# Folding the squares of five norms from four tiles to two on GpSimd, with half the ones-products, two k tiles later

## The chip, the cores and the metric

One core of one Trainium2 chip runs the program. The metric is the device time of one execution in microseconds (us), lower is better. Matrix products run on TensorE (PE in the rows), elementwise work on VectorE (DVE), ScalarE (ACT) and GpSimd (POOL), transfers are issued by SyncE (SP).

## The reference, cut to what matters

Six residual layers run over x of 256 tokens by 1024 features: conformer convolution, forgetting attention, short convolution, conformer convolution again, three attention branches with a gated mix, and a feed-forward layer. Each one norms x, computes, and adds to x:

```python
def rms_norm(x, g):
    xf = x.astype(jnp.float32)
    y = xf * lax.rsqrt(jnp.mean(xf * xf, axis=-1, keepdims=True) + NORM_EPS)
    return (y * g.astype(jnp.float32)).astype(x.dtype)
...
        if kind == 0:
            hn = rms_norm(x, a_norm[j])
            x = x + conformer_conv_mixer(hn, a_w_in[j], a_conv_w[j], a_conv_b[j],
                                         a_ln_g[j], a_ln_b[j], a_w_out[j])
```

What the change touches is `mean(xf * xf)`: a sum of squares over 1024 features for each of 256 tokens. There are six such norms. The first is computed apart; the other five stand at the borders between stages. They are numbered here by their phase: border 1 (into forgetting attention), 2 (into the short convolution), 3 (into the second conformer), 4 (into the three branches), 5 (into the feed-forward layer).

## The kernel before, in words

x is kept transposed in `xT` as eight tiles of 128 features by 256 tokens (k tiles 0 to 7), and worked on in four groups g of two tiles. Every product is made of three fp32r products: the weight is split into a high part `whi` and a low part `wlo`, x into `xh` and `xl`. The weights come in through a ring of three units. A unit is cut into halves; ScalarE makes a half's `whi` (L371), and either VectorE or GpSimd makes its `wlo` (L380). Which of the two it is stands in the half's record, by `cut` (a unit with `ALL` is VectorE's, otherwise the halves alternate). Each engine has its list of instructions in program order; what orders them against each other is semaphores.

At a border this happens. The last output unit's products (L884 to L886) end on TensorE. VectorE adds the result to x (L942) and then folds squares (`rms_fold`, L550: tiles 0 and 1 of `sqb` gather those of groups 0, 1 and 2). ScalarE squares each group (`rms_square`, L542) and makes `xh` of it (`raw_high`, L561); VectorE makes `xl` (`raw_low`, L566). TensorE meanwhile goes on with the next stage's first unit on the x that is not yet normed: `proj_raw` runs three products for each k tile (L752 to L754), after a wait for that tile's `xl`, in a first half (of eight k tiles) and a second one. The norm's factor is applied to the result later. In the middle of the first half stands `rms_pe`: the sum over partitions by fp32 products of a tile of ones with the squares (L720). Out of them ScalarE makes the root (`rms_act`, L697) and VectorE its reciprocal (`rms_dve`, L725), and with it `raw_scale` (L736) and `norm_dve_all` (L730).

Squares of four groups of two tiles are folded by VectorE into tiles 0 and 1; with tiles 6 and 7, the last group, that makes four tiles, and so four products:

```python
            for k in (0, 1, 6, 7):
                if k == 6:
                    pe.wait_ge(sq_done, 4 * ph + k // 2 + 1)
                mm = nc.tensor.matmul(rms_bank[ph][:, 0:S], ones, sqb[:, k, :], start=(k == 0), stop=(k == 7))
```

GpSimd's own list is short: the additions of eleven taps of each convolution (L1120, L1123), the gated product behind it (L1129), and `wlo` of the halves that are its own (`lo_pool_to`). `conf_pool` is its part of a conformer, and begins with `lo_pool_to(pool, last(n["vg"][0][1]))` (L1103), the low halves up to the conformer's first input unit.

Of the kernel before, what the change touches and what calls it, by code (L numbers as in the profile page):

```python
# [20 lines left out]
ALU = mybir.AluOpType  # L21
# [4 lines left out]
S = 256  # L26
TB = S // P
D = 1024
KD = D // P
# [74 lines left out]
def program(nc, t, out):  # L104
    ctx = ExitStack()
    with ctx:
        place = [(nc.sbuf_base + 31) // 32 * 32]

        def sb(name, cols, rows=P, dt=F32):

            at = place[0]
            place[0] += (4 * cols + 31) // 32 * 32
            return nc.alloc_sbuf_tensor_at(name, [rows, cols], dt, offset=at)
# [5 lines left out]
        def sem(name):  # L119
            return ctx.enter_context(nc.semaphore(name))  # L120
# [4 lines left out]
        ones = cst[:, C_ONE:C_ONE + P]  # L125
        blk64 = cst[:, C_B64:C_B64 + P]
        xT = sb("xT", KD * S)[:, :].rearrange("p (k t) -> p k t", t=S)
        sqb = sb("sqb", KD * S)[:, :].rearrange("p (k t) -> p k t", t=S)
# [112 lines left out]
        sq_done = sem("sq_done")  # L241
# [52 lines left out]
        halves = []  # L294
        splits = []
        n_hi = []
        first_half = []
# [19 lines left out]
        def hs(u):  # L317

            return range(first_half[u], first_half[u + 1] if u + 1 < len(first_half) else len(halves))

        def last(u):
            return hs(u)[-1]

        def is_split(h):
            return n_hi[h] > (n_hi[h - 1] if h else 0)
# [61 lines left out]
        def lo_pool_to(pool, h_last):  # L387
            lo_to(pool, nc.gpsimd, pool_at, False, lo_pool, h_last)
# [132 lines left out]
        def plan_ffn(ph):  # L521
            w = t["w_ffn_in_2"][0]
            n = {"ph": ph}
            n["gu"] = [(group((y_raw, 64 + i + 1)), unit_in(w, [(i * P, P), (FF + i * P, P)], ALL)) for i in range(KF)]
            n["out"] = plan_out_ffn(t["w_ffn_out_2"][0])
            return n

        conf0 = plan_conf(0, 0)
        fox = plan_fox(1)
        short = plan_short(2)  # L530
        conf1 = plan_conf(3, 1)
        mixers = plan_mixers(4)
        ffn = plan_ffn(5)
# [3 lines left out]
        rms_bank = [bank[7 if ph in (0, 2) else 3 if ph == 1 else 2] for ph in range(NPH)]  # L537
# [6 lines left out]
        sq_folded = sem("sq_folded")  # L544

        def rms_fold(dve, ph, i):
# [2 lines left out]
            wait(dve, sq_folded, 2 * ph - 1 if i else 0)  # L549
            nc.vector.tensor_tensor(sqb[:, 0:2, :], sqb[:, 0:2, :], sqb[:, 2 * i + 2:2 * i + 4, :], ALU.add).then_inc(sq_folded, 1)  # L550

        RAW = (1, 2, 3, 4, 5)
        RESPLIT = (1, 2, 4, 5)
        RAW_USED = {2: 0, 4: 3, 5: 6}
# [8 lines left out]
        def raw_low(dve, ph, g):  # L563
            for k in (2 * g, 2 * g + 1):
                dve.wait_ge(rh_done, KD * RAW.index(ph) + k + 1)
                nc.vector.scalar_tensor_tensor(xl[:, k, :], xT[:, k, :], norm_g(GAIN[ph], k), xh[:, k, :].bitcast(F32),  # L566
# [146 lines left out]
                                    xh[:, 2 * g:2 * g + 2, :].bitcast(F32), ALU.subtract).then_inc(xn_done, 1)  # L713

        def rms_pe(pe, ph):
            pe.wait_ge(sq_folded, 2 * ph)
            for k in (0, 1, 6, 7):
                if k == 6:
                    pe.wait_ge(sq_done, 4 * ph + k // 2 + 1)
                mm = nc.tensor.matmul(rms_bank[ph][:, 0:S], ones, sqb[:, k, :], start=(k == 0), stop=(k == 7))  # L720
            mm.then_inc(ss_done, 1)

        def rms_dve(dve, ph):
# [18 lines left out]
        def proj_raw(pe, g, u, ph, opens=False, ends=False):  # L742

            b = f_bank if g is None else take_bank(pe, g)
            for a, h in enumerate(hs(u)):
                o = b[:, a * S:(a + 1) * S]
                split_ready(pe, h)
                wh, wl = piece(whi, h), piece(wlo, h)
                for k in range(KD):
                    if opens and a == 0:  # L750
                        pe.wait_ge(rl_done, KD * RAW.index(ph) + k + 1)
                    nc.tensor.matmul(o, wh[:, k, :], xh[:, k, :], start=(k == 0), stop=False)  # L752
                    nc.tensor.matmul(o, wh[:, k, :], xl[:, k, :], start=False, stop=False)
                    mm = nc.tensor.matmul(o, wl[:, k, :], xh[:, k, :], start=False, stop=(k == KD - 1))  # L754
                    if ends and h == last(u) and k in (1, 3, 5):
                        mm.then_inc(raw_used, 1)
                    if opens and a == 0 and k == KD - 3:
                        rms_pe(pe, ph)
                mm.then_inc(half_done, 1)

# [161 lines left out]
        def out_act(act, n):  # L922
            end = n["out"][-1][0]
            for kb, g, u in n["out"]:
                if kb == end and g >= 1:
                    if n["ph"] + 1 in RAW:
                        raw_high(act, n["ph"] + 1, g - 1)
# [173 lines left out]
        def conf_pool(pool, n):  # L1101
            j = n["j"]
            lo_pool_to(pool, last(n["vg"][0][1]))  # L1103
            for c in range(KE):
                first = (j * KE + c) * TAPS_POOL
                for i in range(2, TAPS_POOL):
                    if i == TAPS_POOL // 2 and c + 1 < KE:
                        lo_pool_to(pool, ahead(n["vg"][c + 1][1]))
                    to = accp[:, c % 2, i % 2, :]
                    pool.wait_ge(tmp_done, first + i + 1)  # L1110
                    if i == 2 and c >= 2:
                        if c < 5:
                            pool.wait_ge(raw_done, 3 * j + c - 1)
                        else:
                            pool.wait_ge(conv_done, j * KE + c - 1)
                    if i >= 4:
                        pool.wait_ge(tap_done, first + (1 if i == 4 else 4 if i == 5 else i - 1))
                    a = tmp[:, (first + i - 2) % 4, :] if i < 4 else to

                    nc.gpsimd.tensor_tensor(to, a, tmp[:, (first + i) % 4, :], ALU.add)\  # L1120
                        .then_inc(tap_done, 3 if i == 3 else 1)
                pool.wait_ge(tap_done, first + TAPS_POOL)
                nc.gpsimd.tensor_tensor(accp[:, c % 2, 0, :], accp[:, c % 2, 0, :], accp[:, c % 2, 1, :], ALU.add).then_inc(pool_sum, 1)  # L1123
            for c in range(KE):
                if c in OUT_BESIDE:
                    lo_pool_to(pool, last(n["out"][OUT_BESIDE[c]][2]))
                pool.wait_ge(act_done, j * KE + c + 1)
                wait(pool, sz_done, j * 8 + c // 2 + 1)
                nc.gpsimd.tensor_tensor(y_slot(pool, n["y0"] + c), yb[:, c, :], zb[:, c, :], ALU.mult).then_inc(y_raw, 1)  # L1129
            lo_pool_to(pool, last(n["out"][-1][2]))  # L1130
# [884 lines left out]
        for hh in range(C_SLOTS):  # L2015
            parts = []
            for gi in range(3):
                h = gi * C_SLOTS + hh
# [634 lines left out]
        @block.gpsimd  # L2653
        def _(pool):
            nc.gpsimd.memset(eps, EPS).then_inc(set_pool, 1)
            pool.wait_ge(set_pool, 1)
            nc.gpsimd.memset(small[32:33, 224:224 + HEADS2], 1.0).then_inc(set_pool, 1)
            pool.wait_ge(set_pool, 2)
            conf_pool(pool, conf0)
            lo_pool_to(pool, last(short["out"][-1][2]))  # L2660
            conf_pool(pool, conf1)
            lo_pool_to(pool, len(halves) - 1)

        @block.tensor
# [61 lines left out]
```

## Time and profile before

| what | value |
|---|---|
| median of 3 runs | 1480.84 us (1479.21 to 1481.03) |
| profiled execution, its own time | 1480.18 us |
| its span | 1478.4 us |
| mean granted clock of TensorE | 0.995 |
| TensorE (matmul) busy | 1453.4 us, 98% |
| VectorE busy | 1064.2 us, 72% |
| ScalarE busy | 850.6 us, 58% |
| GpSimd busy | 481.0 us, 33% |

The profile is of one execution; span is from its first to its last instruction, and the 1.8 us between span and time lie around it. An engine's busy time is an average over stages with different limits: what a change is worth at one place is read from that place.

### The profile page before, as it was taken

The page shows a single profiled execution, that of the slowest core. Times are in us where ns is not written, and L with a number is a line of the kernel's source. Part 1 is how long each engine was busy: PE and PEld are TensorE (multiplying, and loading weights), DVE is VectorE, ACT ScalarE, POOL GpSimd, SP SyncE. Part 2 cuts the span into 40 slices and gives each one's busy share as a digit, 9 for nine tenths or more (in the row PEclk, how much of TensorE's full clock was granted, in tenths as well). Part 3 has the DMA queues.
Part 4 walks back from the last instruction along what each step waited for, and adds up shares of the span by engine and source line. Part 5 has one row for each costly group of instructions (what it writes and reads, how often), then busy time and mean ns, then how long its engine had stood idle before and what let it go on. Part 6 is the DMA issues. An engine that isn't in the chain of part 4 may idle for free.

```text
span 1478.4 us, 25122 instructions
## 1 busy us (share of the span) xinstructions
PE 1453.4 (98%) x9279; PEld 1297.1 (88%) x9279; DVE 1064.2 (72%) x2230; ACT 850.6 (58%) x1619; POOL 481.0 (33%) x451
## 2 busy tenths in 40 slices
PE   8999999999999999999999999999999999999998
PEld 6888899998899988889988888989987779988887
DVE  5899767555777798887599997555367778786632
ACT  4567766545666555555456777445456666556542
POOL 2778613433333200000057783064741002000042
PEclk9999999999999999999999999998999999999999
DMA  7554365666654567876455545663852224576653
GB/s 211 150 164 153 119 199 172 230 177 160 122 150 154 151 190 207 216 198 199 144 143 143 143 143 172 186 160 115 220 161 86 83 93 141 157 203 177 186 194 106
DMA packets 308110, 239.40 MB, mean 162 GB/s; under 512 B 18017, under 2 KB 286707, under 8 KB 307988
## 3 DMA queue, kind: packets, MB, share of 16 engines
q1 hardware_dynamic: 295816, 228.70, 53.1%
q10 hardware_dynamic: 12172, 9.10, 2.7%
q8 instruction: 74, 1.21, 0.4%
q14 instruction: 48, 0.39, 0.1%
HBM read 236.02 MB, written 1.75 MB: 161 GB/s over the span
## 4 chain that ended last, share of the span: by engine, by line
PE 66%; DVE 22%; issue 5%; ACT 3%; POOL 2%; DMA 1%; SPq 0%; DVEq 0%; POOLq 0%; ACTq 0%
PE bank L809 12%; DVE bank L1210 11%; PE bank L811 6%; PE bank L884 3%; PE bank L886 3%; PE bank L885 3%; PE bank L1739 3%; PE bank L1740 3%; PE bank L1741 3%; PE bank L787 3%; DVE wlo L380 3%; PE bank L2101 3%; PE bank L1365 2%; PE bank L791 1%; PE bank L906 1%
## 5 line engine op out<-in xcount | busy, mean ns | idle before, releaser
L380 POOL TENSOR_TENSOR wlo<-ring,whi 128x1024 fp32r<-128x1024 f32 x93 | 233.1, 2513 | 842.0 <-ACT whi L371 842.0
L371 ACT CAST whi<-ring 128x1024 fp32r<-128x1024 f32 x336 | 345.0, 1046 | 195.2 <-PE bank L1741 46.3
L380 DVE TENSOR_TENSOR wlo<-ring,whi 128x1024 fp32r<-128x1024 f32 (+1 forms) x243 | 298.1, 1247 | 146.4 <-ACT whi L371 145.7
L787 PE MATMUL bank<-sqb,ring 128*128 128x256 f32 x1504 | 331.9, 380 | 1.1 <-DMA ring<-in_a_w_in_dram 0.9
L787 PEld LDWEIGHTS bank<-sqb,ring 128*128 128x128 f32 x1504 | 283.7, 190 | 47.7 <-issue 6.4
L809 PE MATMUL bank<-xhl,whi 128*128 128x512 f32 x768 | 269.1, 396 | 1.4 <-DVE xhl L712 1.4
L1210 DVE SCALAR_TENSOR_TENSOR bank<-scratch,convw,bank 128x256 f32<-128x256 f32 x600 | 240.5, 483 | 0.0
L1120 POOL TENSOR_TENSOR scratch<-scratch 128x256 f32<-128x256 f32 x288 | 199.8, 730 | 98.3 <-ACT scratch L1062 74.8
L811 PE MATMUL bank<-xhl,wlo 128*128 128x256 f32 x768 | 213.8, 278 | 0.0
L809 PEld LDWEIGHTS bank<-xhl,whi 128*128 128x128 f32 x768 | 144.1, 188 | 36.1 <-issue 2.1
L1062 ACT ACTIVATE scratch<-scratch,convw 128x256 f32<-128x256 f32 x320 | 146.3, 500 | 48.1 <-POOL scratch L1120 47.4
L884 PE MATMUL bank<-y_hi,whi 128*128 128x256 f32 x512 | 146.1, 285 | 1.8 <-DVE wlo L380 1.8
L886 PE MATMUL bank<-y_hi,wlo 128*128 128x256 f32 x512 | 144.9, 283 | 0.0
L885 PE MATMUL bank<-y_lo,whi 128*128 128x256 f32 x512 | 144.8, 283 | 0.0
L811 PEld LDWEIGHTS bank<-xhl,wlo 128*128 128x128 f32 x768 | 144.5, 188 | 0.0
L1739 PE MATMUL bank<-xhl,whi 128*128 128x256 f32 x384 | 110.2, 287 | 0.8 <-DVE qk L1699 0.8
L1740 PE MATMUL bank<-xhl,whi 128*128 128x256 f32 x384 | 108.6, 283 | 0.0
L1741 PE MATMUL bank<-xhl,wlo 128*128 128x256 f32 x384 | 108.6, 283 | 0.0
L884 PEld LDWEIGHTS bank<-y_hi,whi 128*128 128x128 f32 x512 | 98.2, 192 | 2.7 <-ACT whi L371 2.2
L885 PEld LDWEIGHTS bank<-y_lo,whi 128*128 128x128 f32 x512 | 98.2, 192 | 0.1
L886 PEld LDWEIGHTS bank<-y_hi,wlo 128*128 128x128 f32 x512 | 98.2, 192 | 0.0
L1739 PEld LDWEIGHTS bank<-xhl,whi 128*128 128x128 f32 x384 | 73.5, 191 | 3.8 <-issue 2.5
(328 smaller groups left out, 2749.6 us busy)
## 6 DMA issues: line engine op xcount, KB each, us to landing
ring<-in_a_w_in_dram SPq DMA_DIRECT2D x64, 512.0 KB, 5.1
ring<-in_b_w_in_dram SPq DMA_DIRECT2D x32, 1024.0 KB, 6.0
ring<-in_c_w_in_dram SPq DMA_DIRECT2D x64, 512.0 KB, 5.3
ring<-in_w_in_dram SPq DMA_DIRECT2D x26, 1024.0 KB, 5.2
ring<-in_w_ffn_in_dram SPq DMA_DIRECT2D x44, 512.0 KB, 4.9
ring<-in_a_w_in_dram SPq DMA_DIRECT2D x16, 1024.0 KB, 5.1
ring<-in_a_w_out_dram SPq DMA_DIRECT2D x16, 1024.0 KB, 5.3
ring<-in_w_ffn_out_dram SPq DMA_DIRECT2D x10, 1024.0 KB, 5.0
```

The lines of the kernel that those rows point to most:

```text
L371: nc.scalar.copy(piece(whi, h)[:, :, 0:n], src).then_inc(hi_done, 1)
L380: engine.tensor_tensor(piece(wlo, h)[:, :, 0:n], src, piece(whi, h)[:, :, 0:n].bitcast(F32), ALU.subtract).then_inc(done, 1)
L787: mm = nc.tensor.matmul(o, halves[h][1][:, k, :], sqb[:, k, :], start=(k == 0), stop=(k == KD - 1))
L809: nc.tensor.matmul(o[:, :], wh[:, k, :], xhl[:, k, :, :].rearrange("p s t -> p (s t)"), start=(k == 0), stop=False, skip_group_check=True)
L811: mm = nc.tensor.matmul(o[:, 0:S], wl[:, k, :], xh[:, k, :], start=False, stop=(k == KD - 1), skip_group_check=True)
L884: nc.tensor.matmul(o, wh[:, k, :], hi[:, kk, :], start=first, stop=False, skip_group_check=True)
L885: nc.tensor.matmul(o, wh[:, k, :], lo[:, kk, :], start=False, stop=False, skip_group_check=True)
L886: mm = nc.tensor.matmul(o, wl[:, k, :], hi[:, kk, :], start=False, stop=end, skip_group_check=True)
L1120: nc.gpsimd.tensor_tensor(to, a, tmp[:, (first + i) % 4, :], ALU.add)\
L1210: ins = nc.vector.scalar_tensor_tensor(to[:, a, :], src, w, to[:, a, :], ALU.mult, ALU.add)
L1739: nc.tensor.matmul(o, wh, xh[:, k, :], start=first, stop=False, skip_group_check=True)
L1740: nc.tensor.matmul(o, wh, xl[:, k, :], start=False, stop=False, skip_group_check=True)
```

## The change

A new `rms_pairs` on GpSimd adds tile 1 of the squares into tile 0 (after VectorE's second fold), and tile 7 into tile 6 (after ScalarE's last square). TensorE then makes two products with ones in place of four, each after one of these additions, and it makes them behind k tile 7 of the first half, where they stood behind k tile 5. GpSimd's list gets the five calls. Line numbers of the changed kernel are 9 higher from `RAW` to `rms_pe`, 7 higher behind it, and 15 higher at the end.

```diff
+        sq_paired = sem("sq_paired")
+
+        def rms_pairs(pool, ph):
+
+            pool.wait_ge(sq_folded, 2 * ph)
+            nc.gpsimd.tensor_tensor(sqb[:, 0, :], sqb[:, 0, :], sqb[:, 1, :], ALU.add).then_inc(sq_paired, 1)
+            pool.wait_ge(sq_done, 4 * ph + 4)
+            nc.gpsimd.tensor_tensor(sqb[:, 6, :], sqb[:, 6, :], sqb[:, 7, :], ALU.add).then_inc(sq_paired, 1)
+
...
         def rms_pe(pe, ph):
-            pe.wait_ge(sq_folded, 2 * ph)
-            for k in (0, 1, 6, 7):
-                if k == 6:
-                    pe.wait_ge(sq_done, 4 * ph + k // 2 + 1)
-                mm = nc.tensor.matmul(rms_bank[ph][:, 0:S], ones, sqb[:, k, :], start=(k == 0), stop=(k == 7))
+            for i, k in enumerate((0, 6)):
+                pe.wait_ge(sq_paired, 2 * (ph - 1) + i + 1)
+                mm = nc.tensor.matmul(rms_bank[ph][:, 0:S], ones, sqb[:, k, :], start=(k == 0), stop=(k == 6))
             mm.then_inc(ss_done, 1)
...
-                    if opens and a == 0 and k == KD - 3:
+                    if opens and a == 0 and k == KD - 1:
                         rms_pe(pe, ph)
...
             conf_pool(pool, conf0)
+            lo_pool_to(pool, next(h for h in range(first_half[fox["f"]], len(halves)) if is_split(h) and not halves[h][4]))
+            rms_pairs(pool, fox["ph"])
+            lo_pool_to(pool, last(fox["out"][-1][2]))
+            rms_pairs(pool, short["ph"])
             lo_pool_to(pool, last(short["out"][-1][2]))
+            rms_pairs(pool, conf1["ph"])
             conf_pool(pool, conf1)
+            rms_pairs(pool, mixers["ph"])
+            lo_pool_to(pool, last(mixers["out"][-1][2]))
+            rms_pairs(pool, ffn["ph"])
             lo_pool_to(pool, len(halves) - 1)
```

GpSimd's order between the first conformer and the second, before (L1129 is the first conformer's gated product, L380 a low half, L1120 and L1123 the second conformer's taps):

```order
L1120 TENSOR_TENSOR scratch<-scratch 128x256 x9
L1123 TENSOR_TENSOR scratch<-scratch 128x256
L1129 TENSOR_TENSOR yr<-wide 128x256 x16
L380 TENSOR_TENSOR wlo<-ring,whi 128x1024 x41
L1120 TENSOR_TENSOR scratch<-scratch 128x256 x9
L1123 TENSOR_TENSOR scratch<-scratch 128x256
```

and of the change, in the same place (L1136, L1127 and L1130 are the former L1129, L1120 and L1123; L557 and L559 are the two new additions):

```order
L1136 TENSOR_TENSOR yr<-wide 128x256 x16
L380 TENSOR_TENSOR wlo<-ring,whi 128x1024
L557 TENSOR_TENSOR sqb<-sqb 128x256
L559 TENSOR_TENSOR sqb<-sqb 128x256
L380 TENSOR_TENSOR wlo<-ring,whi 128x1024 x39
L557 TENSOR_TENSOR sqb<-sqb 128x256
L559 TENSOR_TENSOR sqb<-sqb 128x256
L557 TENSOR_TENSOR sqb<-sqb 128x256
L559 TENSOR_TENSOR sqb<-sqb 128x256
L380 TENSOR_TENSOR wlo<-ring,whi 128x1024
L1127 TENSOR_TENSOR scratch<-scratch 128x256 x9
L1130 TENSOR_TENSOR scratch<-scratch 128x256
```

The pairs of border 1 stand behind the first of the 41 low halves, those of border 2 behind the 40th. The pairs of border 3 come next, and the 41st low half, which stood right behind the 40th, now stands behind them.

TensorE's order at border 3, before (from the last product of the output to the first k tiles of `proj_raw`; what an instruction waits for stands in brackets):

```order
L886 MATMUL bank7<-y_hi_61,wlo_57 128x256
L752 MATMUL bank0<-xhl_52,whi_56 128x256 [waits lo_pool,rl_done,hi_done,c_cu]
L753 MATMUL bank0<-xhl_52,whi_56 128x256
L754 MATMUL bank0<-xhl_52,wlo_57 128x256
L752 MATMUL bank0<-xhl_52,whi_56 128x256 [waits rl_done]
```

and of the change, from k tile 7 on to the second half:

```order
L759 MATMUL bank0<-xhl_52,whi_56 128x256 [waits rl_done]
L760 MATMUL bank0<-xhl_52,whi_56 128x256
L761 MATMUL bank0<-xhl_52,wlo_57 128x256
L727 MATMUL bank2<-sqb_51,cst_49 128x256 [waits sq_paired] x2
L759 MATMUL bank0<-xhl_52,whi_56 128x256 [waits lo_dve,hi_done]
```

The first half at this border waits for a low half of GpSimd (`lo_pool`), the second for one of VectorE (`lo_dve`), before and after; at the other four borders the first half waits for one of VectorE. The products with ones have moved behind the wait for the last k tile's `xl` (`rl_done`), and wait for the additions.

## Rows read from the trace of the kernel before

**Rows 1.** The page: busy time of each engine, and the chain that ended last.

```profile
PE 1453.4 (98%) x9279; PEld 1297.1 (88%) x9279; DVE 1064.2 (72%) x2230; ACT 850.6 (58%) x1619; POOL 481.0 (33%) x451
...
PE 66%; DVE 22%; issue 5%; ACT 3%; POOL 2%; DMA 1%; SPq 0%; DVEq 0%; POOLq 0%; ACTq 0%
```

**Rows 2.** Timeline of TensorE, border 2: start us, length us, [idle before <-releaser].

```profile
509.84 1.89 PE L720 MATMUL bank<-sqb,cst 128*128 128x256 f32 x8
...
511.69 0.28 PE L753 MATMUL bank<-xhl,whi 128*128 128x256 f32 x1
```

**Rows 3.** Timeline of VectorE, border 2.

```profile
508.49 0.68 DVE L550 TENSOR_TENSOR sqb<-sqb 128x512 f32<-128x512 f32 x1
509.67 0.89 DVE L566 SCALAR_TENSOR_TENSOR xhl<-xT,cols,xhl 128x256 fp32r<-128x256 f32 x2 [0.50 <-ACT xhl L561]
...
513.01 1.75 DVE L725 RECIPROCAL rr<-std 128x256 f32<-128x256 f32 x1
```

**Rows 4.** Timeline of ScalarE, border 2: the last square.

```profile
508.61 0.63 ACT L542 ACTIVATE sqb<-xT 128x512 f32<-128x512 f32 x1
```

**Rows 5.** Timeline of TensorE: its first long waits behind borders 2, 3, 4, 5.

```profile
527.80 0.47 PE L809 MATMUL bank<-xhl,whi 128*128 128x512 f32 x1 [0.48 <-DVE xhl L712]
...
923.24 0.36 PE L884 MATMUL bank<-y_hi,whi 128*128 128x256 f32 x1 [0.90 <-DVE wlo L380]
...
991.66 0.39 PE L791 MATMUL bank<-xhl,whi 128*128 128x256 f32 x1 [1.38 <-DVE xhl L712]
...
1305.43 0.47 PE L809 MATMUL bank<-xhl,whi 128*128 128x512 f32 x1 [0.89 <-DVE xhl L712]
```

**Rows 6.** The chain that ended last, in order of time, border 3.

```profile
737.30 1.74 PE bank L720 x8
...
739.07 0.48 ACT std L697
...
739.64 1.76 DVE rr L725
```

**Rows 7.** Timeline of TensorE, border 3: first half's start, products with ones.

```profile
734.98 0.28 PE L752 MATMUL bank<-xhl,whi 128*128 128x256 f32 x1
...
737.14 1.89 PE L720 MATMUL bank<-sqb,cst 128*128 128x256 f32 x8
```

**Rows 8.** Timelines of GpSimd (first two) and VectorE, border 3.

```profile
728.20 2.49 POOL L380 TENSOR_TENSOR wlo<-ring,whi 128x1024 fp32r<-128x1024 f32 x1 [230.99 <-ACT whi L371]
747.69 0.73 POOL L1120 TENSOR_TENSOR scratch<-scratch 128x256 f32<-128x256 f32 x1 [16.99 <-ACT scratch L1062]
...
728.36 3.02 DVE L566 SCALAR_TENSOR_TENSOR xhl<-xT,cols,xhl 128x256 fp32r<-128x256 f32 x2
...
735.78 0.68 DVE L550 TENSOR_TENSOR sqb<-sqb 128x512 f32<-128x512 f32 x1
736.97 0.88 DVE L566 SCALAR_TENSOR_TENSOR xhl<-xT,cols,xhl 128x256 fp32r<-128x256 f32 x2 [0.50 <-ACT xhl L561]
737.77 1.22 DVE L380 TENSOR_TENSOR wlo<-ring,whi 128x1024 fp32r<-128x1024 f32 x1
```

**Rows 9.** Timelines, first conformer: two GpSimd products of 128x256, a VectorE subtraction between.

```profile
192.19 1.63 POOL L1129 TENSOR_TENSOR yr<-wide 128x256 f32<-128x256 f32 x2 [0.54 <-ACT wide L1091]
...
192.44 0.77 DVE L981 TENSOR_TENSOR y_lo<-yr,y_hi 128x256 fp32r<-128x256 f32 x1 [0.51 <-ACT y_hi L977]
```

**Rows 10.** Stretches: busy us (instructions) of each engine, TensorE's granted clock; a wait.

```profile
1258.00:1261.70 3.70, 1.77 (x15) 1.60 (x14) 3.63 (x6) 0.62 (x1) 0.00 (x0) 1.00 0.28 90
1261.70:1265.10 3.40, 3.40 (x18) 3.40 (x17) 3.25 (x5) 1.57 (x2) 0.00 (x0) 0.50 0.87 293
...
1012.50:1016.00 3.50, 3.50 (x24) 3.44 (x24) 0.00 (x0) 0.00 (x0) 1.75 (x1) 0.50 0.14 23
...
1260.70 0.36 PE L869 MATMUL bank<-m_hl,whi 128*128 128x256 f32 x1 [1.93 <-DVE wlo L380]
```

**Rows 11.** Timeline of VectorE, border 5.

```profile
1287.76 0.89 DVE L566 SCALAR_TENSOR_TENSOR xhl<-xT,cols,xhl 128x256 fp32r<-128x256 f32 x2 [1.32 <-ACT xhl L561]
```

## The prediction

> **What bounds the kernel now.** I read the page first. TensorE is busy for 98% of the span, and the chain that ended last lies on it for 66%, on VectorE for 22% [rows 1]. So work taken off TensorE counts only where TensorE itself is what the next stage waits for. Next come the timelines at the five borders, and there one number matters: the four products with ones. They begin at 509.84, and the second product of the next k tile begins at 511.69 [rows 2]. Products of 256 columns follow each other every 0.12 us (six k tiles of three lie between the two rows of border 3, 2.16 us [rows 7]), so the four took 511.69 - 0.12 - 509.84 = 1.73 us, or 0.43 each. (The eight records are two for each fp32 product, 0.216 apart.) Then I read what VectorE and ScalarE do beside them [rows 3, 4], who is waited for behind each border [rows 5], and for border 3 the chain [rows 6] and GpSimd [rows 8].
>
> The reader should see two things. **First**, behind borders 2 to 5 TensorE's first long waits are for VectorE or for work fed by it: 0.48, 0.90, 1.38 and 0.89 us [rows 5]. There TensorE's time saved at the border only lengthens the wait. **Second**, at border 3 the products with ones stand in the chain: ones, root, reciprocal, each at once behind the other [rows 6], and VectorE's convolution follows.
>
> **The change part by part.**
>
> *Two products fewer.* 5 borders by 2 by 0.43 = 4.3 us of TensorE's work. That is all it could save.
>
> *Two k tiles later.* At border 2 TensorE is through with k tile 5 at 509.84 [rows 2]. `xl` of k tiles 6 and 7 is made by the two L566 from 509.67 on, ending about 510.15 and 510.56 [rows 3]. Before, the products with ones covered that. Now TensorE must wait for k tile 6 to 510.2 and for 7 to 510.6. Its products then take 0.36 and the two with ones 0.86: first half done at 511.9, before at 509.84 + 1.73 + 0.72 = 512.3. Of the 0.86 saved, 0.4 is left, even if nothing else happens.
>
> *GpSimd's additions.* One addition of 128x256 takes 0.73 us [rows 8], two in a row 1.43. The first can start when L550 ends, 509.17 at border 2 [rows 3], the second when the last square ends, 509.24 [rows 4]. They would run to 510.7, under the two L566. Here the rows speak against the change: GpSimd and VectorE exclude each other when VectorE reads two tiles of SBUF. The subtraction L981 issued at 192.44 under GpSimd's product of 192.19 took 0.77, and the two GpSimd products 1.63 [rows 9]. Two L566 under a low half of GpSimd took 3.02 [rows 8], where 0.88 is usual. So addition and `xl` take turns: addition 1 to 509.97, tile 6 to 510.25, addition 2 to 510.76, tile 7 to 511.04. VectorE is 0.48 late. Bounds: nothing, if they don't exclude each other, and 0.82, if both additions go first (tile 7 at 511.4). I take 0.48, the order of rows 9. The Trainium skill (GPSIMD Engine Reference, Key points) says that GpSimd shares its SBUF interfaces with VectorE, with contention where an instruction has two SBUF inputs; by that rule the sum below stands, and without it the sum would be 2.0 us smaller (0.5 at borders 1, 2 and 4, 0.3 at border 3, 0.2 at border 5). The trace agrees with the rule here.
>
> With that, TensorE ends border 2's first half at 511.1 + 0.36 + 0.86 = 512.3, as before: the gain is gone. VectorE's chain to the wait at 527.80 (its low halves, reciprocal at 513.01 without a wait, scaling) moves by 0.5.
>
> *Border 1* has the same times within 0.05, but no wait on VectorE for a long stretch: TensorE +0.1. *Border 4*: as border 2, +0.5 at 991.66. *Border 5*: `xl` is made later, from 1287.76 [rows 11]; addition 1 is over by then and only the second is met: VectorE +0.2, and so the wait at 1305.43.
>
> *Border 3, the low half that moved.* The order shows that the 41st low half of GpSimd now stands behind the pairs of border 3. It is that of the second conformer's first half, which TensorE starts at 734.98 [rows 7] with a wait for it. Before it was made at 728.20, 4 us ahead [rows 8]. Now: L550 ends at 736.46 [rows 8]; addition 1 to 737.26; addition 2, in turn with L566, to 738.05; the low half waits for the second L566 to 738.33 and takes 2.4, to 740.7. TensorE starts at 740.8: **5.8 us idle**. Eight k tiles take 24 by 0.12 = 2.9, to 743.7. From the first product with ones to the root it was 739.07 - 737.14 = 1.93 [rows 6, 7]; with four records fewer it is 1.93 - 0.86 = 1.07, so the root starts at 744.7, **5.7 us late**. VectorE waited for that root (reciprocal at 739.64, right behind it [rows 6]), and from there the convolution runs on VectorE, ScalarE and GpSimd up to TensorE's wait of 0.90 at 923.24 [rows 5]. TensorE is as late as they are, so nothing absorbs it: +5.7. VectorE's low half of the second TensorE half (737.77 [rows 8]) is pushed to about 741.8, still before 743.7.
>
> *The clock.* After TensorE's wait of 1.93 us ending at 1260.70, its granted clock was 0.50, 1.2 GHz, for 3.4 us [rows 10]. In it 18 matmuls were made where 28 fit at 0.12: 1.2 us lost. A wait of 5.8 should do the same, and the first half that follows is on the path. I take +1.2; bounds are nothing (the low clock falls wholly in the wait) and 3.1, if it stays low through the whole first half and the ones, as it stayed low for longer from 1012.5 on [rows 10]. The Trainium skill (TensorE: Matmul & The Clock Gate, Part 1: The HAM clock gate) has an idle TensorE fall back to half rate; a drop to 1.2 GHz after border 3 follows from it as from the rows, and without it the sum would be 1.2 less.
>
> **The sum**: 0.1 + 0.5 + (5.7 + 1.2) + 0.5 + 0.2 = **+8.2 us**. Against the profiled execution's 1480.2 that is 1488.4. The median of the runs is 0.7 above the profiled one, so I predict 1489.0 for the median.
>
> **Rivals.**
>
> *The saving comes through*: no waits on `xl`, no low half late, VectorE not behind: 1480.8 - 4.3 = 1476.5. For it speaks TensorE's 98%. Against it, four waits on VectorE [rows 5] and `xl` of tile 6 not there at 509.84 [rows 3]. It would also need the low half of border 3 to be another one than I read. Chance 0.03.
>
> *Only turns and waits*: the late low half costs nothing (the half needed is another, or its wait is taken up by slack of the convolution). Then borders 1, 2, 4, 5 give +1.3, and at border 3 the root comes 0.8 later (tile 7 at 738.33, 0.36 and 1.07 behind it, so 739.8 for 739.07): 1480.8 + 2.1 = 1482.9, no measurable change. Against it: the first half waits for GpSimd in the order, and VectorE's chain has no slack there. Chance 0.06.
>
> *The late low half is worse*: GpSimd, waiting behind L566, loses the turn to VectorE's own low half (1.14 us), the clock is low for all of the first half, and both additions go first elsewhere. 8.2 + 1.1 + 1.9 + 3 by 0.3 = +12.1: 1492.9. Chance 0.13. *Milder*: no exclusion and no low clock, 8.2 - 2.0 - 1.2 = +5.0: 1485.8, chance 0.13. *As forecast*, within 2 us of 1489.0: 0.65. The three together are slower, 0.91.
>
> **How the numbers follow.** The range reaches from the mild case, less a spread of 0.9 as the runs of before show it, 1485.0, to the bad case, 1493.5; what is left out is the two other cases and a rest. About 0.2% (3 us) is what a measurement can tell from no change here: faster by more 0.03, within it 0.06, slower by more 0.91.
>
> **What would show it right or wrong.** In the changed kernel's timeline of TensorE: at border 3 a wait of about 5.8 us before the first L759, released by GpSimd's L380; at the other borders short waits on L566 before k tiles 6 and 7; the four records of L727 then 0.86 shorter. In VectorE's timeline: L566 of 0.6 to 0.9 us where it was 0.48, and the reciprocal at border 3 some 6 to 7 us later than border 3 begins. In the clock: a fall to 0.50 in or right behind the long wait. The end of the first four borders' stages should lie 0.1, 0.6, 7.5 and 8.0 us later. Wrong would be: no wait at border 3, or one that TensorE makes up before 923, or L566 of 0.48 under GpSimd's additions.

## The result and the profile after

The changed kernel takes 1490.66 us (median of 6 runs, 1486.75 to 1493.74); the kernel before took 1480.93 beside it (median of 6). The ratio is 1.007, 95% interval 1.0052 to 1.0087: 0.7% slower, some 10 us. One of the six of the kernel before took 2122.22 us; it counts as slow and isn't in the ratio, which is of fast runs. A second measurement gave 1491.71 against 1481.93, ratio 1.0071 (1.0053 to 1.0088). The profiled execution has a span of 1487.2 us, before 1478.4, and a mean granted clock of 0.993.

The page of the changed kernel, busy time and chain, against [rows 1]:

```profile
span 1487.2 us, 25092 instructions
...
PE 1452.0 (98%) x9259; PEld 1295.9 (87%) x9259; DVE 1066.5 (72%) x2230; ACT 850.5 (57%) x1619; POOL 487.5 (33%) x461
...
PE 66%; DVE 22%; issue 5%; ACT 3%; POOL 2%; DMA 1%; SPq 0%; DVEq 0%; POOLq 0%; ACTq 0%
```

On this page almost nothing has changed. TensorE is 1.4 us less busy, the shares are the same within a point, and the time is 10 us longer. The time has to be looked for at the borders. Border 3 comes first. TensorE (against [rows 7]):

```profile
741.36 0.55 PE L759 MATMUL bank<-xhl,whi 128*128 128x256 f32 x1 [5.73 <-POOL wlo L380]
...
746.14 1.03 PE L727 MATMUL bank<-sqb,cst 128*128 128x256 f32 x4
```

GpSimd at the same border (against the first of [rows 8]):

```profile
737.04 0.72 POOL L557 TENSOR_TENSOR sqb<-sqb 128x256 f32<-128x256 f32 x1 [226.27 <-DVE sqb L550]
737.72 0.90 POOL L559 TENSOR_TENSOR sqb<-sqb 128x256 f32<-128x256 f32 x1
738.59 2.51 POOL L380 TENSOR_TENSOR wlo<-ring,whi 128x1024 fp32r<-128x1024 f32 x1
```

VectorE and ScalarE:

```profile
735.67 0.69 DVE L949 TENSOR_TENSOR xT<-bank,xT 128x512 f32<-128x512 f32 x1 [3.28 <-PE bank L893]
736.28 0.68 DVE L550 TENSOR_TENSOR sqb<-sqb 128x512 f32<-128x512 f32 x1
737.46 1.45 DVE L575 SCALAR_TENSOR_TENSOR xhl<-xT,cols,xhl 128x256 fp32r<-128x256 f32 x2 [0.50 <-ACT xhl L570]
738.83 3.35 DVE L380 TENSOR_TENSOR wlo<-ring,whi 128x1024 fp32r<-128x1024 f32 x1
...
747.78 1.75 DVE L732 RECIPROCAL rr<-std 128x256 f32<-128x256 f32 x1 [5.44 <-ACT std L706]
...
747.20 0.47 ACT L706 ACTIVATE std<-bank,small 128x256 f32<-128x256 f32 x1 [8.08 <-PE bank L727]
```

The low half that the first half needs was made at 728.20 before; here it starts at 738.59, behind the two additions. GpSimd had been idle for 226 us ahead of them. TensorE waits 5.73 us, makes its first half, then the products with ones, and only then come the root and the reciprocal. The clock in three stretches of this border (same columns as [rows 10]):

```profile
736.00:738.70 2.70, 0.00 (x0) 0.00 (x0) 2.20 (x4) 2.29 (x4) 1.66 (x3) 1.00 0.00 0
738.70:745.50 6.80, 4.14 (x19) 4.17 (x20) 3.64 (x6) 0.42 (x1) 2.40 (x1) 0.50 0.31 90
745.50:750.00 4.50, 4.50 (x35) 4.22 (x33) 2.19 (x3) 1.76 (x2) 0.00 (x0) 1.00 0.38 99
```

Within TensorE's wait the granted clock falls to 0.50 (1.2 GHz) and stays there for 6.8 us; TensorE is busy for 4.14 us of that.

Border 2 on TensorE (against [rows 2] and the first of [rows 5]), then GpSimd, VectorE and ScalarE (against [rows 3, 4]):

```profile
510.23 0.39 PE L759 MATMUL bank<-xhl,whi 128*128 128x256 f32 x1 [0.32 <-DVE xhl L575]
...
511.11 0.39 PE L759 MATMUL bank<-xhl,whi 128*128 128x256 f32 x1 [0.26 <-DVE xhl L575]
...
511.57 1.03 PE L727 MATMUL bank<-sqb,cst 128*128 128x256 f32 x4
...
528.30 0.47 PE L816 MATMUL bank<-xhl,whi 128*128 128x512 f32 x1 [0.48 <-DVE xhl L721]
```

```profile
509.17 0.73 POOL L557 TENSOR_TENSOR sqb<-sqb 128x256 f32<-128x256 f32 x1 [12.04 <-DVE sqb L550]
509.85 0.92 POOL L559 TENSOR_TENSOR sqb<-sqb 128x256 f32<-128x256 f32 x1
...
507.80 0.69 DVE L949 TENSOR_TENSOR xT<-bank,xT 128x512 f32<-128x512 f32 x1 [1.13 <-PE bank L893]
...
509.58 1.47 DVE L575 SCALAR_TENSOR_TENSOR xhl<-xT,cols,xhl 128x256 fp32r<-128x256 f32 x2 [0.50 <-ACT xhl L570]
510.98 2.35 DVE L380 TENSOR_TENSOR wlo<-ring,whi 128x1024 fp32r<-128x1024 f32 x2
...
513.51 1.75 DVE L732 RECIPROCAL rr<-std 128x256 f32<-128x256 f32 x1
...
512.63 0.48 ACT L706 ACTIVATE std<-bank,small 128x256 f32<-128x256 f32 x1 [1.38 <-PE bank L727]
```

The two L575 take 1.47 where they took 0.89: they take turns with the additions. TensorE stops for the low part (0.32 us) ahead of k tile 6 and again (0.26) ahead of 7. The later waits of TensorE, against the last three of [rows 5] (that at 997.21 has no counterpart there):

```profile
931.31 0.36 PE L891 MATMUL bank<-y_hi,whi 128*128 128x256 f32 x1 [0.90 <-DVE wlo L380]
...
997.21 0.36 PE L798 MATMUL bank<-xhl,whi 128*128 128x256 f32 x1 [0.63 <-DVE xhl L721]
...
1001.10 0.38 PE L798 MATMUL bank<-xhl,whi 128*128 128x256 f32 x1 [1.51 <-DVE xhl L721]
...
1315.32 0.47 PE L816 MATMUL bank<-xhl,whi 128*128 128x512 f32 x1 [0.86 <-DVE xhl L721]
```

**A ledger by border.** To compare kernels I measure, within each execution, from the start of a border's last addition to x to a landmark, a wait of TensorE that every kernel has: at border 1 a wait of 0.28 us at 331.32, at borders 2 to 5 those of [rows 5]. What drifted ahead of the border drops out. In experiments 7 to 9 VectorE's second fold stands ahead of that addition. At border 5, where VectorE was idle for only 0.24 us there, this makes the addition itself late: it starts 0.72 to 0.75 us behind the start of TensorE's last output product, in all other kernels 0.32. In those three the ledger of border 5 therefore starts 0.32 behind that product. For border 3 before, the addition starts at 735.18 and the wait ends at 923.24: 188.06. After, 735.67 and 931.31: 195.64, which is 7.6 longer. "Root" is the same for the start of the root on ScalarE. Differences to the kernel before, in us (the numbers are those of the experiments below):

| kernel | 1 | 2 | 3 | 4 | 5 | sum | median, ratio (95%) |
|---|---|---|---|---|---|---|---|
| the change | +0.22 | +0.59 | +7.57 | +1.38 | +0.16 | +9.9 | 1.007 (1.0052, 1.0087) |
| its root | +0.94 | +0.95 | +7.64 | +0.95 | +0.95 | | |
| 6 the change, second trace | +0.23 | +0.60 | +7.93 | +1.97 | +0.19 | +10.9 | 1.0071 (1.0053, 1.0088) |
| 1 half first | +0.24 | +0.59 | +0.88 | +1.48 | +0.16 | +3.4 | 1.0023 (1.0011, 1.0035) |
| 3 late place only | +0.57 | +0.57 | +1.16 | +0.94 | +0.76 | +4.0 | 1.0031 (1.0017, 1.0046) |
| 4 additions only | 0.00 | +0.58 | +0.09 | +0.56 | +0.15 | +1.4 | 1.0009 (0.9995, 1.0024) |
| 5 early place | -0.12 | +0.59 | +0.10 | +2.04 | +0.16 | +2.8 | 1.0020 (1.0007, 1.0032) |
| 2 late half only | 0.00 | +0.02 | +6.81 | +0.01 | +0.02 | +6.9 | 1.0042 (1.0025, 1.0058) |
| 7 three products | -0.44 | +0.01 | -0.42 | +0.07 | +0.02 | -0.8 | 0.9980 (0.9969, 0.9990) |
| 8 three, high first | -0.43 | -0.51 | -0.41 | -0.54 | -0.49 | -2.4 | 0.9973 (0.9963, 0.9984) |
| 9 fold earlier only | 0.00 | +0.01 | +0.01 | -0.03 | -0.01 | 0.0 | 1.0009 (0.9997, 1.0021) |
| 10 high first only | 0.00 | -0.51 | 0.00 | -0.45 | -0.53 | -1.5 | 1.0005 (0.9995, 1.0016) |

The stretches between the borders are not in the ledger. Two of them are equal in all thirteen traces within 0.03 us. The other four vary from execution to execution: up to border 1 (237.1 to 239.9 us), from the landmark of border 2 to border 3 (207.4 or 210.4), from the landmark of border 4 to border 5 (290.5 to 294.0), and behind the last landmark (169.6 to 170.7). Medians are of 7 to 12 runs (6 for the change, each time), each beside the kernel before (24 to 33 runs, 6 in the first measurement).

### The profile page after: what moved, and what is told of

Its sections match the earlier page's. It is cut to its first block, busy times and chain, and to the rows that moved or that the text cites. A ratio compares the mean times of both kernels' runs of the same rounds, so it can differ in the third digit from the quotient of the medians.

```text
span 1487.2 us, 25092 instructions
## 1 busy us (share of the span) xinstructions
PE 1452.0 (98%) x9259; PEld 1295.9 (87%) x9259; DVE 1066.5 (72%) x2230; ACT 850.5 (57%) x1619; POOL 487.5 (33%) x461
## 4 chain that ended last, share of the span: by engine, by line
PE 66%; DVE 22%; issue 5%; ACT 3%; POOL 2%; DMA 1%; SPq 0%; DVEq 0%; POOLq 0%; ACTq 0%
PE bank L816 12%; DVE bank L1217 11%; PE bank L818 6%; PE bank L891 3%; PE bank L893 3%; PE bank L892 3%; PE bank L1746 3%; PE bank L1747 3%; PE bank L1748 3%; PE bank L794 3%; PE bank L2108 3%; DVE wlo L380 3%; PE bank L1372 2%; PE bank L798 1%; PE bank L913 1%
## 5 line engine op out<-in xcount | busy, mean ns | idle before, releaser
L380 POOL TENSOR_TENSOR wlo<-ring,whi 128x1024 fp32r<-128x1024 f32 x93 | 232.1, 2502 | 529.4 <-ACT whi L371 529.3
L380 DVE TENSOR_TENSOR wlo<-ring,whi 128x1024 fp32r<-128x1024 f32 (+1 forms) x243 | 300.0, 1256 | 145.4 <-ACT whi L371 144.7
L1127 POOL TENSOR_TENSOR scratch<-scratch 128x256 f32<-128x256 f32 x288 | 199.5, 729 | 95.9 <-ACT scratch L1069 72.4
L816 PEld LDWEIGHTS bank<-xhl,whi 128*128 128x128 f32 x768 | 144.3, 188 | 35.3 <-issue 2.0
L557 POOL TENSOR_TENSOR sqb<-sqb 128x256 f32<-128x256 f32 x5 | 3.7, 731 | 317.2 <-DVE sqb L550 317.2
```

The costliest lines, as they stand in the source:

```text
L380: engine.tensor_tensor(piece(wlo, h)[:, :, 0:n], src, piece(whi, h)[:, :, 0:n].bitcast(F32), ALU.subtract).then_inc(done, 1)
L816: nc.tensor.matmul(o[:, :], wh[:, k, :], xhl[:, k, :, :].rearrange("p s t -> p (s t)"), start=(k == 0), stop=False, skip_group_check=True)
```

## The experiments

**1. The 41st low half ahead of the pairs of border 3.** All else as in the change.

```diff
+            lo_pool_to(pool, last(conf1["vg"][0][1]))
             rms_pairs(pool, conf1["ph"])
             conf_pool(pool, conf1)
```

> The change, with GpSimd's 41st low half put back ahead of the pairs of border 3. Theory (the late half is the loss): no TensorE wait on GpSimd at border 3 (5.73 us in the change), no fall of the clock there; the root at border 3 comes 0.8 us later than in the kernel before, not 7.6; total 2.3 us above the kernel before (borders 1 to 5: 0.2, 0.6, 0.8, 0.5, 0.2), some 7.5 us below the change. Rival one (turns between GpSimd and VectorE and the late place are the loss): still 6 us or more above the kernel before. Rival two (two products fewer pay once the half is in time): 4 us below the kernel before.

Measured: 1482.95 us against 1480.43, ratio 1.0023. Border 3 falls from +7.57 to +0.88. The low half is made early again, and TensorE has only the two short waits of the other borders:

```profile
734.00 2.49 POOL L380 TENSOR_TENSOR wlo<-ring,whi 128x1024 fp32r<-128x1024 f32 x1 [220.98 <-ACT whi L371]
...
743.41 0.39 PE L759 MATMUL bank<-xhl,whi 128*128 128x256 f32 x1 [0.32 <-DVE xhl L575]
...
744.29 0.39 PE L759 MATMUL bank<-xhl,whi 128*128 128x256 f32 x1 [0.25 <-DVE xhl L575]
```

One call in another place is worth 6.7 us of the change's 10. What is left, +0.23% (0.11 to 0.35), is still a loss.

**2. The late low half alone.** The kernel before, with GpSimd held ahead of it until the last square; no addition, four products, the old place.

```diff
+            pool.wait_ge(sq_done, 4 * conf1["ph"] + 4)
             conf_pool(pool, conf1)
```

> The kernel before with one wait more: GpSimd waits for the last square of border 3 before it makes its 41st low half. No additions, four products, old place. Theory (the late half alone): the low half starts 2 us earlier than in the change, since no additions stand before it, so TensorE waits 4.1 us for it, the two L566 are held behind it, the root comes 4.1 us later and 1 to 2 more by a fall of the clock: 4.5 to 6 us above the kernel before. Rival (the second conformer has slack): under 2 us.

Measured: 1487.60 against 1481.93, ratio 1.0042. Border 3 alone moves, by 6.8:

```profile
740.19 2.34 POOL L380 TENSOR_TENSOR wlo<-ring,whi 128x1024 fp32r<-128x1024 f32 x1 [242.43 <-ACT sqb L542]
...
742.79 0.55 PE L752 MATMUL bank<-xhl,whi 128*128 128x256 f32 x1 [4.07 <-POOL wlo L380]
...
749.44 0.47 ACT L697 ACTIVATE std<-bank,small 128x256 f32<-128x256 f32 x1 [7.23 <-PE bank L720]
...
741.40:748.20 6.80, 5.41 (x22) 5.17 (x23) 3.10 (x7) 0.81 (x1) 1.13 (x1) 0.50 0.40 114
```

A wait of 4.07 us costs 6.8. The low clock again lasts 6.8 us, but here 5.41 us of it fall on a busy TensorE, in the change 4.14. From TensorE's first product to the root it takes 749.44 - 742.79 = 6.65 where it was 739.07 - 734.98 = 4.09 [rows 6, 7]: 2.6 lost to the low clock, where the change lost 1.9. TensorE itself starts 4.2 later, measured against the addition, and 4.2 + 2.6 = 6.8. The shorter wait has the dearer clock behind it. The expectation had the wait right and the clock too small (1 to 2): 6.8 lies above its 4.5 to 6, the median's 5.7 inside.

**3. The late place alone.** The kernel before with one number changed.

```diff
-                    if opens and a == 0 and k == KD - 3:
+                    if opens and a == 0 and k == KD - 1:
```

> The kernel before, with its four products with ones behind k tile 7 instead of 5; no additions on GpSimd. Theory: TensorE waits 0.3 and 0.4 us for xl of k tiles 6 and 7 at each border, and the root comes 1.15 us later; VectorE's L566 stay at 0.48. Total 3.5 us above the kernel before (0.4 on TensorE at border 1; VectorE's reciprocal 0.45, 1.15, 0.7 and 0.7 later at borders 2 to 5). Rival (the place costs nothing, as the wait is hidden): the same as before.

Measured: 1484.06, ratio 1.0031, ledger +4.0. It was expected at 3.5, and the medians give 3.6. The root comes 1.2 to 1.3 later at borders 1 to 4 and 1.6 at border 5. Of this 0.72 are the two k tiles that now stand ahead of it, and the rest is waiting for `xl`. So the place, with nothing gained in return, costs 4 us; in the change the two saved products hide part of that.

**4. The additions alone.** The kernel before, and GpSimd makes the ten additions into two tiles of `yr` that nothing uses at that time and nobody reads; VectorE waits for them ahead of the reciprocal. The 41st low half stays ahead of the pairs, as in experiment 1. It adds work and leaves nothing out.

```diff
+            nc.gpsimd.tensor_tensor(yr[:, 0, :], sqb[:, 0, :], sqb[:, 1, :], ALU.add).then_inc(sq_paired, 1)
+            pool.wait_ge(sq_done, 4 * ph + 4)
+            nc.gpsimd.tensor_tensor(yr[:, 1, :], sqb[:, 6, :], sqb[:, 7, :], ALU.add).then_inc(sq_paired, 1)
```

> The kernel before with its four products at their old place, and GpSimd's two additions at each border into spare tiles, read by nobody (the low half of border 3 in time). It adds work and leaves nothing out. Theory (GpSimd and VectorE take turns): the pair of L566 takes 1.45 us where it was 0.88, and VectorE is 0.5 us later behind borders 2 and 4, 0.2 behind 5; at border 3 its wait for the root of 0.5 us swallows it, at border 1 too; total 1.2 us above the kernel before. Rival (turns cost nothing on the path): the same as before, though L566 are longer.

Measured: 1481.58, ratio 1.0009 (0.9995 to 1.0024): by the median it can't be told from nothing. The trace can tell it. VectorE at border 2, with the additions at 509.77 and 510.46:

```profile
510.19 1.46 DVE L575 SCALAR_TENSOR_TENSOR xhl<-xT,cols,xhl 128x256 fp32r<-128x256 f32 x2 [0.50 <-ACT xhl L570]
```

The pair takes 1.46 without any other part of the change, and the landmarks move by 0.58, 0.56 and 0.15 at borders 2, 4 and 5, where VectorE leads to them, and by nothing at 1 and 3.

**5. The pairs in the old place.** Experiment 1 with the two products behind k tile 5, as before.

```diff
-                    if opens and a == 0 and k == KD - 1:
+                    if opens and a == 0 and k == KD - 3:
```

> The change with the low half in time and its two products put back behind k tile 5. Theory: TensorE waits for GpSimd's second addition instead (0.2 and 0.4 us), xl of tiles 6 and 7 is hidden again, the root comes 0.3 us earlier than in the kernel before; VectorE is still 0.5, 0.5 and 0.2 late behind borders 2, 4 and 5. Total 0.9 us above the kernel before, 1.4 below the half-first kernel. Rival (late place was harmless): equal to the half-first kernel.

Measured: 1482.85, ratio 1.002, ledger +2.8. The expectation (+0.9, and 1.4 below experiment 1) failed: by the medians this kernel equals experiment 1 (1482.95), as its rival had it. The root is 0.13 earlier than before (borders 1 to 4) where 0.3 was expected, although two products of 0.43 are gone. The second product has to wait for the second addition:

```profile
512.48 0.70 PE L727 MATMUL bank<-sqb,cst 128*128 128x256 f32 x2 [0.17 <-POOL sqb L559]
```

In the old place the second addition is not ready, in the late one two k tiles stand ahead. Either way the addition of tile 7 into 6 gives nothing, because it stands between the last square and the root. At border 4 this kernel lost 2.04 where 0.5 was expected, which is most of the miss; see point 4 below.

**6. The change once more.**

> The change as it is, beside the kernel before on this chip. Theory: 9 to 10 us above the kernel before, of which 5.7 are TensorE's wait for the low half at border 3 and 1.9 the low clock behind it, the rest the five borders' late place and turns. Rival (its gap over the half-first kernel is chance): within 5 us of the kernel before.

Measured: 1491.71 against 1481.93 (24 runs), ratio 1.0071. The size stands. Its trace has the same wait at border 3 (5.73) and the same low clock (6.8 us). The clock fell later within the wait, and TensorE needed 5.05 us to the products with ones where the first trace has 4.78: 2.2 lost for 1.9.

**7. Three products.** The fault of the second addition suggests another kernel. GpSimd adds only tile 1 into tile 0. VectorE's second fold goes ahead of the last addition to x, so that this addition has time. Tiles 6 and 7 keep a product each, behind k tile 5, and the 41st low half stays first.

```diff
+            pool.wait_ge(sq_folded, 2 * ph)
+            nc.gpsimd.tensor_tensor(sqb[:, 0, :], sqb[:, 0, :], sqb[:, 1, :], ALU.add).then_inc(sq_paired, 1)
...
-            pe.wait_ge(sq_folded, 2 * ph)
-            for k in (0, 1, 6, 7):
+            pe.wait_ge(sq_paired, ph)
+            for k in (0, 6, 7):
...
+                    if g == 3:
+                        rms_fold(dve, n["ph"] + 1, 1)
```

> VectorE's second fold stands ahead of the last x addition, where VectorE is idle; GpSimd adds tile 1 into tile 0 then, ahead of L566; three products with ones behind k tile 5, tiles 6 and 7 unpaired; low half of border 3 in time. Theory: no turns with L566 (0.88 for the pair), no waits on xl, TensorE and the root 0.43 us earlier at each border; that counts at border 1 (0.4) and in the root at border 3 (0.4), not where VectorE ends last: 0.9 us below the kernel before. Rival (GpSimd's additions cost wherever they stand): 1 us or more above.

Measured: 1479.06 against 1481.93, ratio 0.9980 (0.9969 to 0.9990). The ledger has 0.4 at borders 1 and 3, one product each, as expected, and nothing at 2, 4 and 5, where VectorE decides. The median gained 2.9 where the ledger has 0.8.

**8. Three products, high part first.** Where VectorE decides, it waits 0.50 for ScalarE's `xh` [rows 3], which stands behind the last square. Now it stands ahead.

```diff
         def rms_act(act, ph):
-            rms_square(act, ph, 3)
             raw_high(act, ph, 3)
+            rms_square(act, ph, 3)
```

> As the three-products kernel, and ScalarE makes xh of the last group before its square. Theory (borders 2, 4 and 5 hang on VectorE's xl, which waits 0.5 us for xh): xl and VectorE's chain 0.5 us earlier at borders 2 and 4, about 0.2 at border 5, beside the 0.4 at borders 1 and 3: 2 us below the kernel before. Rival (those borders hang on TensorE): no better than the three-products kernel.

Measured: 1477.39 against 1481.93, ratio 0.9973 (0.9963 to 0.9984). Borders 2, 4 and 5 now gain too, by 0.5 each. The ledger's -2.4 is what experiments 7 (-0.8) and 10 (-1.5) have together. This is the fastest of the kernels here, so it was measured a second time:

> Three products with GpSimd adding only tile 1 into tile 0, the earlier fold and the high part first, once more beside the kernel before. The first time its ratio was 0.9973 (about -4 us), its timeline accounted for -2.8. If the ledger is right 0.998; if something beyond it pays each time, 0.997 again.

Measured: 1477.63 against 1479.44, ratio 0.9981 (0.9968 to 0.9995). That is 1.8 us, the ledger's size (-2.3 in this trace) and not the 4 to 5 us of the first time. The 2.8 in the expectation was measured from the late addition of border 5; it is 2.4. GpSimd, VectorE and ScalarE at its border 2:

```profile
507.91 0.74 POOL L557 TENSOR_TENSOR sqb<-sqb 128x256 f32<-128x256 f32 x1 [10.34 <-DVE sqb L550]
...
508.24 0.69 DVE L951 TENSOR_TENSOR xT<-bank,xT 128x512 f32<-128x512 f32 x1 [0.41 <-PE bank L893]
509.51 0.88 DVE L573 SCALAR_TENSOR_TENSOR xhl<-xT,cols,xhl 128x256 fp32r<-128x256 f32 x2 [0.58 <-ACT xhl L568]
...
508.96 0.91 ACT L568 ACTIVATE xhl<-xT,cols 128x256 fp32r<-128x256 f32 x2
509.78 0.61 ACT L542 ACTIVATE sqb<-xT 128x512 f32<-128x512 f32 x1
```

The addition (507.91) lies under the last addition to x and is over before the `xl` pair, which takes its old 0.88. The addition to x is not slowed: 0.69 as before. It reads one operand from a bank.

**9. The earlier fold alone**, on the kernel before, with four products.

```diff
+                    if g == 3:
+                        rms_fold(dve, n["ph"] + 1, 1)
```

> The kernel before with one edit: VectorE makes its second fold of squares (L550) ahead of the last addition to x, where it stands behind it. Four products with ones, GpSimd adds nothing. The run with three products, which has this edit too, measured 2.9 us below the kernel before, where its timeline accounts for 0.4 at borders 1, 3 and 5 each (1.2). Theory A (the saved product is what paid): the last x tiles are then made 0.68 later and the last xl with them, but the fold no longer stands between the addition and xl, so nothing on the path moves by over 0.1 at a border: 0, within 0.2 us of 1.000 by ratio 0.9995 to 1.0005. Theory B (the earlier fold paid for most): ratio 0.998 as with three products. A takes from the ledger, B from the median.

Measured: 1481.09 against 1479.44, ratio 1.0009 (0.9997 to 1.0021). Theory B falls: the earlier fold is not what paid in experiment 7. VectorE at border 5:

```profile
1284.29 0.69 DVE L550 TENSOR_TENSOR sqb<-sqb 128x512 f32<-128x512 f32 x1
1284.89 0.68 DVE L944 TENSOR_TENSOR xT<-bank,xT 128x512 f32<-128x512 f32 x1
```

TensorE's last output product started at 1284.17, so the addition comes 0.72 behind it, without an idle gap. The landmark is where it was against that product. The 0.4 at border 5 and the sum of 1.2 that the expectation ascribes to experiment 7 come from this late addition; without it the sum is 0.8.

**10. The high part first, alone**, on the kernel before: the diff is that of experiment 8.

> The kernel before with one edit: ScalarE makes the high part of the last group ahead of its last square (raw_high ahead of rms_square in rms_act). Nothing else moves. The last square then ends some 0.45 us later, 509.7 at border 2, still ahead of TensorE's products with ones at 509.84, so the root stays. VectorE waited 0.50 us for the high part ahead of its last two L566; that wait goes. Where VectorE's chain leads to TensorE's next wait (borders 2, 4, 5), that gives 0.5 each; at borders 1 and 3 the root decides and nothing moves. Theory: -1.5 us, ratio 0.999. Rival: the square is late for the third product at some border, +0.1 to 0.3 there, and the sum is -0.5 to -1.

Measured: 1481.26 against 1479.44, ratio 1.0005 (0.9995 to 1.0016). The ledger has the expected gains at borders 2, 4 and 5 (-1.5), but the median does not show them. The low end of the interval is -0.7 us. In the profiled execution (1481.10 us, before 1480.18) the stretches outside the ledger more than make up for them: +1.8 ahead of border 1, +3.0 behind border 2, -1.7 ahead of border 5, -0.7 behind it. Whether that is so in the twelve runs isn't shown. So for differences of 1 or 2 us ledger and median need not agree in this kernel, and of the 2.9 of experiment 7 only 0.8 is explained. That the combination of experiment 8 is faster rests on its two intervals.

## Why the prediction was right

It gave 1489.0, range 1485.0 to 1493.5, slower by over 0.2%. The measured 1490.66 lies inside, 9.7 above the kernel before where 8.2 was forecast. The two terms that were off, the clock and border 4, were both too small, so the sum isn't right because errors cancelled. Step by step:

1. **The products.** They save what was reckoned: the four records of L727 start at 746.14 and the root at 747.20, 1.06 later, forecast 1.07. Nothing of it reached the end: in no border of the ledger is the change faster.
2. **Turns of GpSimd and VectorE** (forecast 0.48 for the pair). Measured 1.47 - 0.89 = 0.58; tile 7's `xl` was forecast for 511.04 and TensorE's k tile 7 started at 511.11, in an execution that reached the border 0.09 earlier. Borders 2 and 5 gave 0.59 and 0.16 (forecast 0.5 and 0.2). Experiment 4 shows them with the additions alone, so the mild rival (no exclusion) is out. At border 1 the forecast was 0.1, measured 0.22.
3. **Border 3.** The wait of 5.8 was 5.73, and experiments 1 and 2 show the late low half as its cause, by taking it away (-6.7) and by making it alone (+6.8). The reckoned path held too: root late, reciprocal 5.44 idle behind it, nothing made up by 931. **The clock term was mis-sized**: I took 1.2 from the 3.4 us after a wait of 1.93 [rows 10]. Two of the 18 products counted there had begun earlier; 16 began in it, 0.213 apart for 0.12, which is 1.5 lost. And the low clock lasted twice as long, 6.8 us, and from TensorE's start to the products with ones it was 746.14 - 741.36 = 4.78 where 2.9 was reckoned: 1.9. It lies between the bounds given (0 and 3.1). With it, border 3 is 5.7 + 1.9 = 7.6, the ledger's 7.57.
4. **Border 4** was forecast at +0.5 "as border 2" and measured +1.38. There 0.58 is VectorE's, as expected (experiment 4 has 0.56). The other 0.8 I did not see: the norm's high parts on ScalarE stand behind a `whi` that waits for a transfer, and this wait grew from 4.53 to 5.36 us. In the changed kernel:

```profile
993.03 1.05 ACT L371 CAST whi<-ring 128x1024 fp32r<-128x1024 f32 x1 [5.36 <-DMA ring<-in_w_in_dram]
993.98 2.17 ACT L717 CAST xhl<-sqb 128x512 fp32r<-128x512 f32 x4
```

It was 5.45 in experiment 1, 6.00 in experiment 5 and 6.00 in the second trace of the change, the others with a high border 4 (+1.48, +2.04, +1.97), and 4.43 in the additions alone (+0.56). SyncE issued that transfer at 978.42 before and at 987.03 after; from there to the `whi` it was 983.58 - 978.42 = 5.16 and 993.03 - 987.03 = 6.00. So the transfer itself was 0.84 slower to land. The same stretch is 6.0 to 6.6 us in the four traces with two products and 5.1 to 5.4 in the nine others. The DMA queues in it (packets, MB, share), first the change, then the kernel before:

```profile
q1 hardware_dynamic: 1040, 1.05, 55.4%
q8 instruction: 1, 0.02, 1.3%
```

```profile
q1 hardware_dynamic: 1040, 1.05, 65.8%
```

In the change one packet of 16 KB of an instruction queue falls into this transfer. So it does in all four slow traces. In the nine others the last such packet starts 2.4 to 5.8 us before the transfer is issued, and none falls into it. That makes it the likely cause. It is not shown to be one, as no run moved that packet alone.

5. **The rivals.** "The saving comes through" and "only turns and waits" (1482.9) needed a harmless low half. Experiment 1 is that second case made real: 1482.95 - 1480.43 = +2.5, where the rival had +2.1 (by the ledger border 3 +0.9 for 0.8, border 4 +1.5 for 0.5). The worse case failed in its first part: GpSimd, starting at 738.59, did not lose its turn to VectorE's low half. VectorE's took 3.35 and waited for GpSimd's 2.51. Its second part, the low clock for all of the first half, came in the main: 4.14 of the 4.78 us, for 1.9 and not 3.1.

The sum by the ledger is 9.9 where 8.2 was forecast: +0.9 from border 4, +0.7 from the clock, +0.2 from borders 1 and 2.

## What to carry to other kernels

An engine that looks idle for 226 us may still have one instruction whose time matters: before you put waiting work into its list, look at what stands next behind it and who waits for that. Work taken off the busiest engine pays only if its replacement is finished before the old work would have been; fold the part whose operands are ready early (0.4 us here, at two of five borders) and leave the last-made part alone. Price an idle TensorE by its wait and by what it does after it, since the low clock (6.8 us here) lands on that work.

## What the runs showed of the hardware

- **A shorter wait can lose more to the low clock than a longer one.** After waits of 5.73 and 4.07 us the granted clock was 0.50 for 6.8 us both times, after 1.93 for 3.4 [rows 10]. In the first two it fell while TensorE still waited, at 738.7 and 741.4, and the longer wait covered more of it. The wait of 1.93 itself had no fall behind it in three of the thirteen traces (experiments 1 and 5, and the second of 8). And the clock fell at 1012.5 [rows 10] although TensorE had been busy in all of the 3.5 us before, for the most part with products of 30 columns:

```profile
1009.00:1012.50 3.50, 3.50 (x35) 2.79 (x27) 1.20 (x3) 2.02 (x3) 0.91 (x2) 1.00 0.74 259
```

- **GpSimd and VectorE take whole instructions in turn.** Additions of 0.73 us become 0.90 and the pair of `xl` 1.46 for 0.88 with both there; VectorE's low half of 1.22 took 3.35 over GpSimd's of 2.51. The addition to x, one operand in a bank, ran beside GpSimd's addition at its usual 0.69 (experiment 8).
- **Spread of 3 us outside the borders, from more than one source.** In seven of thirteen profiled executions (experiments 1 to 4, 8 twice, and 10) the stage behind border 2 took 3.0 us longer at a granted clock of 1.00, whatever the edit: TensorE's products follow each other a little slower there, 120 us holding 341 of the wide ones for 347. TensorE, grouped by form, 560 to 680, first the kernel before, then experiment 10:

```profile
L809 PE MATMUL bank<-xhl,whi 128*128 128x512 f32 x347 | 120.3, 393 | 0.0
```

```profile
L809 PE MATMUL bank<-xhl,whi 128*128 128x512 f32 x341 | 120.5, 399 | 0.0
```

What decides it isn't known. Another source lies between the landmark of border 4 and border 5, and there the time goes with how long the granted clock was 0.50: 290.5 and 291.4 us with 6.8 us of it (the second traces of the change and of experiment 8), 291.8 to 292.5 with 10.2 (experiments 1, 2, 5, 9, 10 and the first of 8), 293.5 to 294.0 with 13.7 (the kernel before, the change, experiments 3, 4 and 7). A third, ahead of border 1 (237.1 to 239.9 us), is not taken apart. This is why spans of single executions mislead here by more than the effects of most of these experiments, and why they are compared by border and by medians.
